# A linear-attention mixer on one core: level scores placed between two projections, and two orders changed on GpSimd and VectorE

## What is computed

```python
q, fp, i_in, gate = jnp.split(h @ w_in, 4, axis=-1)      # h 528 x 1024, w_in 1024 x 8192
q = silu(q); f = lb + (1 - lb) * sigmoid(fp); log_f = log(f); k = (1 - lb) * sigmoid(-fp)
# per head: S_t = diag(f_t) S_{t-1} + k_t i_t^T,  o_t = S_t^T q_t
o = o * rsqrt(mean(o * o) + EPS) * o_norm
y = (o * silu(gate)) @ w_out
```

## Time and profile before

| | us |
|---|---|
| median of 3 runs | 3217.63 |
| lowest, highest | 3217.52, 3218.79 |
| the profiled execution's own time | 3220.95 |
| its span, first to last instruction | 3219.2 |
| mean granted TensorE clock over the span | 0.887 |

### The profile page before, as it was taken

The page is one execution under the profiler, slowest core; times in us unless marked ns, Lnnn a source line. Parts: engine busy times, 40 slices in busy tenths (PEclk is TensorE's granted clock), DMA queues, the critical chain, the costliest instruction groups (busy, mean ns, idle before and its releaser), DMA issues. The chain is left out here.

```text
span 3219.2 us, 36203 instructions
## 1 busy us (share of the span) xinstructions
PE 2555.9 (79%) x12276; PEld 1759.3 (55%) x12276; DVE 2108.6 (66%) x3964; ACT 997.9 (31%) x2010; POOL 1170.2 (36%) x952
## 2 busy tenths in 40 slices
PE   6998969999999968767799688966766677766676
PEld 5998959889988858324466533322322232222222
DVE  6356646666666675466534327788887788878876
ACT  2222145555555521232223212222222222222221
POOL 2443345555455522011100214444444444444442
PEclk8999988889898979878899899998888888888888
DMA  3233621111111034100110249999999999999998
GB/s 99 87 95 99 190 59 50 43 52 46 52 52 46 27 122 140 39 28 0 40 40 1 79 171 400 415 427 427 410 427 426 423 403 427 427 420 402 427 423 341
DMA packets 269757, 666.41 MB, mean 207 GB/s; under 512 B 13989, under 2 KB 201546, under 8 KB 203834
## 3 DMA queue, kind: packets, MB, share of 16 engines
q0 software_dynamic: 73728, 536.90, 39.9%
q1 hardware_dynamic: 194906, 127.75, 13.2%
q10 hardware_dynamic: 992, 0.13, 0.0%
HBM read 662.64 MB, written 2.10 MB: 206 GB/s over the span
## 5 line engine op out<-in xcount | busy, mean ns | idle before, releaser
L1898 PE MATMUL peer_py<-peer_uv,peer_diag 128*128 128x512 f32 x1536 | 852.0, 703 | 348.4 <-ACT peer_diag L1828 348.2
L1616 POOL DMA_INDIRECT peer_uv<-k_peer_uv,peer_idx x512 | 510.8, 998 | 773.3 <-PE peer_py L1898 710.7
L1898 PEld LDWEIGHTS peer_py<-peer_uv,peer_diag 128*128 128x128 f32 x1536 | 324.4, 223 | 842.2 <-issue 835.1
L1718 DVE SCALAR_TENSOR_TENSOR peer_spare<-peer_uv,peer_hp 128x1024 bf16<-128x1024 f32 x512 | 622.8, 1217 | 226.2 <-DMA peer_uv<-k_peer_uv,peer_idx 225.4
L1820 ACT ACTIVATE peer_ga<-peer_a 128x2 f32<-128x2 f32 x256 | 52.0, 203 | 827.3 <-DVE peer_spare L1718 827.3
L862 PE MATMUL hgrn_pp<-p2n_hh,hgrn_wh 128*128 128x264 f32 x1024 | 227.2, 305 | 27.6 <-POOL hgrn_wl L733 27.6
L733 POOL TENSOR_TENSOR hgrn_wl<-p2n_w,hgrn_wh 128x1024 fp32r<-128x1024 f32 x64 | 153.8, 2403 | 183.7 <-ACT hgrn_wh L770 183.7
L862 PE MATMUL hgrn_pp<-p2n_hl,hgrn_wh 128*128 128x264 f32 x1024 | 218.6, 296 | 0.0
L862 PE MATMUL hgrn_pp<-p2n_hh,hgrn_wl 128*128 128x264 f32 x1024 | 217.2, 295 | 0.0
L862 PEld LDWEIGHTS hgrn_pp<-p2n_hh,hgrn_wh 128*128 128x128 f32 x1024 | 171.7, 204 | 28.8 <-POOL hgrn_wl L733 28.2
L1828 ACT ACTIVATE peer_diag<-keep_ident,peer_wt 128x128 f32<-128x128 f32 x384 | 140.3, 396 | 113.7 <-DVE peer_wt L1725 109.8
(11 more groups left out here) (371 smaller groups left out, 4850.4 us busy)
## 6 DMA issues: line engine op xcount, KB each, us to landing
p2n_w<-in_hgrn_w_in SPq DMA_DIRECT2D x64, 512.0 KB, 3.9
p1n_w<-in_pool_w_in SPq DMA_DIRECT2D x32, 512.0 KB, 3.9
pool_out_aw<-in_w_ada SPq DMA_DIRECT2D x16, 768.0 KB, 4.7
hgrn_out_aw<-in_w_ada SPq DMA_DIRECT2D x16, 768.0 KB, 4.7
pool_out_w<-in_pool_w_out SPq DMA_DIRECT2D x8, 1024.0 KB, 7.0
hgrn_out_w<-in_hgrn_w_out SPq DMA_DIRECT2D x8, 1024.0 KB, 7.3
p_w<-in_w_pq SPq DMA_DIRECT2D x8, 1024.0 KB, 6.3
peer_uv<-k_peer_uv,peer_idx POOLq DMA_INDIRECT x512, 12.1
```

The lines of the kernel that those rows point to most:

```text
L1616: pool.indirect_dma_start(out=uv[:, n % DEPTH].rearrange("p w d -> p (w d)"), out_offset=None, in_=io["k_peer_uv"], in_offset=bass.Indirec ...
L1718: dve.scalar_tensor_tensor(out=spare[:, n % 2, :], in0=uv[:, n % DEPTH, 0, :], scalar=1.0, in1=hp[:, t % 2, :], op0=ALU.mult, op1=ALU.mult ...
L1898: last = pe.matmul(py[:, h * 512:(h + 1) * 512], diag[:, products(n) % DIAGS, :], uv[:, n % DEPTH, 1, h * 512:(h + 1) * 512], start=n % (P ...
```

## The change

Four edits, all in `hgrn_phase`. On GpSimd, `low(I)` is moved from between levels 2 and 3 to before level 0. On TensorE, `project` can do half of its chunks, and the level scores are put between halves: before, GATE, levels 3 to 7, `added_state`, I; now first half of GATE, levels 3 and 4, second half of GATE, levels 5 and 6, first half of I, level 7, `added_state`, second half of I. On VectorE the order of differences (d) and masks (m) is changed, and `to_end` (e) comes before the last two masks. No instruction's shape changes, and their number in the steps is the same.

```diff
@@ GpSimd
             def step(n, b, ahead):
                 if ahead >= 1:
                     low(n + 1, GATE)
-                    levels(n + 1, 1 - b, range(0, 3))
                     low(n + 1, I)
-                    levels(n + 1, 1 - b, range(3, NS))
+                    levels(n + 1, 1 - b, range(NS))
@@ TensorE
-            def project(n, part):
+            def project(n, part, begin=0, end=KC):
                 slot = part % 2
-                pe.wait_ge(wl_done, n * 4 + (part + 1))
...
+                if begin == 0:
+                    pe.wait_ge(wl_done, n * 4 + (part + 1))
...
-                for c in range(KC):
+                for c in range(begin, end):
...
-                last.then_inc(projected, 1)
+                if end == KC:
+                    last.then_inc(projected, 1)
@@ TensorE, step
-                if ahead >= 1:
-                    project(n + 1, GATE)
-                if has(n, 0):
-                    for l in range(3, NL):
-                        scores(n, b, l)
-                    added_state(n)
-                if ahead >= 1:
-                    project(n + 1, I)
+                for part, levels in ((GATE, (3, 4)), (GATE, (5, 6)), (I, (7,)), (I, ())):
+                    if ahead >= 1:
+                        begin = 0 if levels in ((3, 4), (7,)) else KC // 2
+                        project(n + 1, part, begin, begin + KC // 2)
+                    if has(n, 0):
+                        for l in levels:
+                            scores(n, b, l)
+                        if 7 in levels:
+                            added_state(n)
@@ VectorE, step
-                for kind, l in ("d2", "d3", "d4", "m3", "m4", "d5", "m5", "m6", "d6", "m7"):
+                for kind, l in ("d2", "d3", "m3", "m4", "d4", "d5", "m5", "d6", "e7", "m6", "m7"):
                     if kind == "d" and ahead >= 1:
                         difference(n + 1, int(l))
+                    if kind == "e" and ahead >= 1:
+                        to_end(n + 1)
                     if kind == "m" and has(n, 0):
                         mask(n, int(l))
-                if ahead >= 1:
-                    to_end(n + 1)
```

More of the change, by code:

```diff
@@ L850, in _ @@
         def _(pe):
-            def project(n, part):
+            def project(n, part, begin=0, end=KC):
                 slot = part % 2
-                pe.wait_ge(wl_done, n * 4 + (part + 1))
[L854 to L858, removed]
-                for c in range(KC):
+                if begin == 0:
+                    pe.wait_ge(wl_done, n * 4 + (part + 1))
+                    if part == Q:
+                        if has(n, 1):
+                            pe.wait_ge(vt_done, n)
+                    elif part != F or has(n, 1):
+                        pe.wait_ge(proj_taken, n * 4 + (part - 1))
+                for c in range(begin, end):
                     for j, (x, y) in enumerate(((wh, hh), (wh, hl), (wl, hh))):
```

## The result

The changed kernel takes **3191.49 us** (median of 6 runs, 3189.24 to 3201.83), against 3217.57 for the kernel before in the same comparison; ratio 0.9924, 95% interval 0.9911 to 0.9937. It is faster by 26 us where I forecast 84, and lies outside my range of 3122 to 3157.

A forecast was written before the change was run, and what follows sets the result against it. TensorE was taken as the bound, through a mask-product wait and the lower clock behind it. 606.9 - 14 x 37.5 = 81.9, plus 1.7, plus 0.5: 84 us off 3217.63, so 3134 us, range 3122 to 3157.

The forecast's parts named there:

- What bounds the kernel: Mixer steps of 43.35 us: TensorE sets the pace, losing 3.03 us to a mask-product wait and running at lower clock behind it.
- TensorE's own work, 37.1, with seams 37.5: One mixer step on TensorE at full clock without waits: 37.1 us, plus 0.3 to 0.4 for four added seams.
- The low part of I in GpSimd's hole: Its 2.34 us fit GpSimd's idle time behind ScalarE's cast; 0.7 delay on VectorE's difference of level 2, none on the step.
- The low part of the next F comes earlier too: On GpSimd at about 33 to 35.4 us of the step, beside VectorE's `hats` products, holding them 2.1 at worst.
- The loop of VectorE and ScalarE: Their work per step: 12.5 + 11.6 + 7.7 + 3.1 = 34.9 us, against TensorE's 37.5.
- The first rival: VectorE and ScalarE become the bound, held by two low parts: steps of 38.2 to 39.1, 3144 to 3156 us; chance 0.18.
- The clock: TensorE's clock should stay up in the mixer steps with no gap of the old size left: the other half of the gain.
- the third rival: `scaled` ends too late, TensorE waits 3 us for the squares, clock falls: step 44.7, 3236 us; chance 0.03.
- VectorE's new order: VectorE's differences and masks laid out per step: level 7 has 3.6 us to spare, the states a shortest cover of 1.7.
- Ends of the phase: First and last mixer steps: 0.5 us gained at the start, 1.7 at step 14's squares.

The follow-up runs named there:

- e_scaled_first: The changed kernel with VectorE doing `scaled` of the head behind ahead of `hats` of the next; 3129.1 us, 0.9719 of the kernel before.
- e_no_dve: The changed kernel without VectorE's new order, GpSimd's and TensorE's edits kept; 3154.3 us, 0.9796 of the kernel before.
- e_pool_only: The kernel before with GpSimd's edit alone, the low part of I ahead of all levels; 3184.9 us, 0.9893 of the kernel before.
- e_low_after_hats: The changed kernel, but GpSimd waits for `hats` before the low parts of the next F and Q; 3148.6 us, 0.9776 of the kernel before.
- e_end_last: The changed kernel with VectorE's end differences behind the last mask again; 3167.4 us, 0.9837 of the kernel before.
- e_gap_l7: e_scaled_first, but TensorE's level 7 waits for the mask product of level 6 instead of 5; 3172.2 us, 0.9852 of the kernel before.

## Why the prediction was wrong

**What bounds the kernel** was read rightly: a wait of 3 us for a mask product, held by the low part of I, and the clock behind it. That wait went, and so did its loss.

**TensorE's own work, 37.1, with seams 37.5:** right, if 0.4 to 0.8 too long. e_scaled_first runs at 37.2 with 0.5 of waiting for the states in it, so the added seams cost nothing that can be seen.

**The low part of I in GpSimd's hole:** right in place. It came right behind ScalarE's cast and ended 0.31 us ahead of the first level (821.78 to 824.18, level 0 at 824.49). The addition of mask 2 beside it took 2.24 us where the one of mask 1 took 0.43: a hold of 1.8 where I allowed 2.1, and TensorE did not wait for it.

**The failed step is the next one: "The low part of the next F comes earlier too ... beside VectorE's products for `hats`. Held at worst by 2.1."** The prediction puts only F there and gives the low part of Q no place. In the kernel before the two lay 5.1 us apart, both behind `hats`:

```profile
858.15 2.40 POOL L733 TENSOR_TENSOR hgrn_wl<-p2n_w,hgrn_wh 128x1024 fp32r<-128x1024 f32 x1 [2.92 <-ACT hgrn_wh L770]
863.26 2.38 POOL L733 TENSOR_TENSOR hgrn_wl<-p2n_w,hgrn_wh 128x1024 fp32r<-128x1024 f32 x1 [2.72 <-ACT hgrn_wh L770]
```

In the changed kernel ScalarE's cast of Q ended at 840.66, before GpSimd was through with F at 840.83, so the two low parts ran on without a gap and each held one product: 5.3 us from the start of the first product to the reciprocal (838.70 to 844.00) where it was 1.1 (855.90 to 857.01), a hold of 4.2 and not 2.1.

The loop of VectorE and ScalarE, cut as in the prediction, measures 11.9 + 12.8 + 11.9 + 3.2 = 39.8 in the step from 812.65 us, where I had 12.5 + 11.6 + 7.7 + 3.1 = 34.9. The third term, from the states to the end of `scaled`, has all of the 4.2; the others are 0.6 less, 1.2 more and 0.1 more. So the loop passed TensorE's 37.5, and 39.8 is what a step takes where the clock stays up. The first rival's 39.1 is 34.9 with two holds, but it counted the low part of I as one of them. That its number came close is in part luck.

**The clock:** I wrote that it should stay up if no such gap is left. The gap of 3.2 ahead of the squares was the third rival's, and the clock fell in most steps; but the stretch at the low level cost 2.4 to 3.7 us (42.2 to 43.5 against 39.8) and not the 4.2 that I had taken from the one of 8.5 us. So this rival came out on the fast side, and the result is rival 1 with a part of rival 3. I had given them 0.18 and 0.03 as if they excluded each other. They are one chain: once the loop is the bound, TensorE waits for the squares, and that wait is a gap that can cost the clock.

**VectorE's new order** I costed by its masks and states alone. Its effect through ScalarE on the start of the low parts, 2.6 us, was not a term of the sum, though the prediction did place the low part of F beside `hats`.

**Ends of the phase:** VectorE's second `gates` came 1.2 us earlier (479.31 against 480.50), for the 0.5 that I took. From the last `gates` to the squares of step 14 it is 32.6 us (1060.70 to 1093.30) against 35.8, a gain of 3.2 for the 1.7 that I took. With the 25.5 of the 14 steps that is 29.9 of the 30.2 us between the two profiled executions.

## What to carry to other kernels

An engine off the path that gets ahead can be worse than one that is late: lay its instructions beside those of the engine with which it contends, and count every one that can follow without a gap, not the first alone. Where two such pairs must meet, let the one that is held be work that nobody waits for; here a swap of two calls turned 26 us of gain into 91, each against the kernel before in its own comparison. And an edit's worth is not its own: the same VectorE order cost 37 us beside one arrangement and gave 24 beside the other.

## What the runs showed of the hardware that I had not expected

- VectorE's `TENSOR_TENSOR` with two SBUF inputs is held for the rest of GpSimd's `TENSOR_TENSOR` (0.70 becomes 2.70, 0.57 becomes 2.76), two in a row by two in a row; the reciprocal with one input is not (3.44 beside two low parts, 3.45 before). The `SCALAR_TENSOR_TENSOR` of `scaled` is held too (0.77 before, 2.81 beside the low part of Q in e_no_dve, at 820.32). This agrees with the rule of the Trainium skill, page "SBUF — State Buffer", section "SBUF: two separate sides", that the prediction gives.
- A gap of 1.42 us behind 4 us of 64-column score matmuls cost TensorE's clock in every step of e_pool_only. Gaps of 1.0 (e_low_after_hats) and 1.2 (e_no_dve) behind the output matmuls and transposes did not: both stayed at 1.00 over 570 us. A gap of 1.3 at that same place in e_end_last, with waits of 0.25 and 0.47 us shortly ahead of it, did in four of 14 steps. And gaps of 2.1 (e_gap_l7) and 3.2 (the changed kernel) did not in every step. So no length of gap found here parts those that cost the clock from those that do not.
